# Value pages of a paged sample attention asked for by GpSimd's queue instead of SyncE's

## Chip, cores and metric

The kernel runs on one core of a Trainium2 chip. The metric is the device time of one execution in microseconds (us); the median of three runs of the kernel before is 1930.12 us (1930.09 to 1933.59). A core has TensorE (PE; its weight loads are listed as PEld), VectorE (DVE), ScalarE (ACT), GpSimd (POOL) and SyncE (SP), which here does nothing but ask for transfers and wait. The transfers run on 16 DMA engines.

## The reference, cut to what matters

One inference step of a small decoder: a gated short convolution layer, then a "forgetting attention" layer that reads shared keys and values, each followed by a gated embedding, and a last norm. There is a prompt of 1024 rows and a *sample* part: 8 sequences (batches) of 8 new rows each, which attend to 1024 cached rows apiece. The cached keys and values lie in a pool of pages of 128 rows; a page table names the eight pages of each batch. The change lies in the sample attention alone:

```python
k_past = cache_k[page_table].reshape(db, -1, N_HEADS, HEAD_DIM)      # 8 batches x 8 pages x 128 rows
v_past = cache_v[page_table].reshape(db, -1, N_HEADS, HEAD_DIM)
...
s_past = jnp.einsum('bqhd,bkhd->bhqk', q, k_past).astype(jnp.float32) * scale
s_past = s_past + cn_q + jnp.swapaxes(rest, 1, 2)[:, :, None, :]     # sums of log forget values
...                                                                  # s_new: against the 8 new rows, causal
p = jax.nn.softmax(jnp.concatenate([s_past, s_new], axis=-1), axis=-1)
o = jnp.einsum('bhqk,bkhd->bqhd', p[..., :P].astype(v_past.dtype), v_past)
o = o + jnp.einsum('bhqk,bkhd->bqhd', p[..., P:].astype(v_new.dtype), v_new)
```

All inputs and outputs are fp32. A page of keys, and one of values, is 128 rows x 1024 numbers: 512 KB.

## The kernel before, in words

Each engine has a program of its own, written out by hand; they are ordered by semaphores (`wait_ge`, `then_inc`). An instruction of an engine that waits holds up all behind it on that engine. The stages are: convolution layer, first embedding, keys and values, prompt attention (8 head pairs), **sample attention**, output projection, second embedding, norm. The sample attention goes from about 1449 to 1675 us of the profiled execution.

*Buffers of the sample attention.* `Kr` ("Kpages") holds eight key pages, `Vb` ("Vpages") eight value pages: one batch of each, and slot `pg` is used again for page `pg` of the next batch. `RB` holds the bias rows of two batches.

*TensorE, per batch b* (`sample_batch`, line 899): it turns key pages 3 to 7 with the identity (`k_turn`, line 808; the transposes are line 814), each in two halves, and between them forms the scores of finished pairs of pages (`s_scores`, line 833). `s_new` adds the scores against the new rows (lines 824 to 847). Then it turns pages 0 and 1 of batch b+1, turns the softmax weights of batch b (`s_p_turn`, lines 859 and 862), and multiplies them with the values (`s_values`, line 878: two halves of the heads, nine groups of four products each, the first eight groups over the value pages in their order, the ninth over the new rows). At its end it counts `s_pv`. Then come page 2 of batch b+1, the biases of batch b+1, and the transposes of the result (line 886).

*VectorE and ScalarE, per batch:* each copies one half of every turned key page out of PSUM (`keep_keys`: DVE line 1560, ACT line 1193). VectorE takes the maxima of the two halves of the heads (line 1578), with the copy of key page 0 of batch b+1 between the first and the second, and the copy of page 1 behind the second; ScalarE takes the exponentials (line 1207), one for each half. Then both copy the turned weights (lines 1591, 1216 and 1218), and VectorE scales the result (line 1599).

*SP, per batch* (`batch_pages`, line 431): first `value_pages(b)`, which loads the number of a page from the table into a register (`page`, line 292), waits once until the values of batch b-1 are done (`s_pv`, line 428), and asks for eight value pages (line 429). Behind it, for each of the eight key pages of batch b+1, it loads the page number, waits until TensorE has turned the page of batch b that lies in that slot (`s_kturn`), and asks (line 437). Then it asks for the bias rows of batch b+2 once the scores of batch b are done. After the seventh round it asks for the first two blocks of `w_out_b` (line 301), for the values of batch 7, and for the parked prompt output `Y` (line 451); once batch 7 is done it asks for `X` (line 456) and the remaining weights.

*The counters.* Those named in `LEAD` begin at the number written there, so that `START[name] + n` means "n more than at the start". `y_out` and `kv_out` say that the stores of the prompt attention have landed, whose SBUF the value pages take over.

*GpSimd* scales weights and softmax rows in the earlier stages, writes constants into `RB` before the sample attention (lines 561 to 565), and then has nothing to do until the last norm (line 569, from about 1800 us).

Of the kernel before, what the change touches and what calls it, by code (L numbers as in the profile page):

```python
# [27 lines left out]
SEQ, DB, DS = 1024, 8, 8  # L28
# [4 lines left out]
NPAIR = H // 2  # L33
PAGES, PAGE = 8, 128
# [50 lines left out]
START = {name: n for per in LEAD.values() for name, n in per.items()}  # L85


def f(x):

    return x.bitcast(F32)  # L90


def program(nc, a, o, d):

    es = ExitStack()
    with es:
        def sb(ctx, name, shape, dt=F32):
            return ctx.enter_context(nc.sbuf_tensor(name, shape, dt))

        def sem(name):  # L100
            return es.enter_context(nc.semaphore(name))
# [14 lines left out]
        pt = sb(es, "pt", [1, DB * PAGES], I32)  # L116
# [84 lines left out]
        Vb = sb(s2, "Vpages", [P, PAGES, D])  # L201
# [15 lines left out]
        def score_bank(qb):  # L217
# [2 lines left out]


        names = (
            "const_ready sp_step in_rows in_bf in_x0 in_x1 in_x2 w_in0 w_in1 w_gained w_hi w_split block_done act_evac dve_evac "
            "h_hi h_ready g_turned g_ready x_turned x_first x_act x_dve x_sum x_parked x_back y_back y_merged out_dma "
            "uc_turned uc_act uc_out f_raw f_abs f_ln f_lf f_turned f_nat f_aug f_augdma "
            "staged kv_turned kv_nat kv_out kq_hi kq_lo v_hi v_lo z_done "
# [7 lines left out]
        sems = {k: sem(k) for k in names}  # L234
# [19 lines left out]
        cv = a["cache_v"].rearrange("n s h d -> (n s) (h d)")  # L254
        cl = a["cache_logf"].rearrange("n s h -> (n s) h")
        last_page = a["cache_k"].shape[0] - 1
# [18 lines left out]
        def _(sp):  # L275
# [15 lines left out]
            def page(b, pg):  # L291
                v = sp.value_load(pt[0:1, bass.ds(PAGES * b + pg, 1)], min_val=0, max_val=last_page)  # L292
                return bass.ds(v * PAGE, PAGE)

            def load(n, par, src, proj=None, cols=P):

                sp.wait_ge(sems["w_split"], START["w_split"] + n - 1)
                sp.sem_inc(sems["sp_step"], 1)
                if proj is None:
                    for c in (0, 4):  # L300
                        sp.dma_start(raw[:, par, c:c + 4, 0:cols], src[:, c:c + 4, :]).then_inc(sems[f"w_in{par}"], 16)
                else:
                    sp.dma_start(raw[:, par, 0:KC, :], src).then_inc(sems[f"w_in{par}"], 16)
                    sp.dma_start(raw[:, par, KC:, :], proj).then_inc(sems[f"w_in{par}"], 16)
# [63 lines left out]
            def load_rest(b, par):  # L368
                for c in range(2):
                    sp.dma_start(f(RB[H * c:H * c + H, par, :]), d["rest"][bass.ds(H * b, H), c, :]).then_inc(sems[f"s_restin{par}"], 16)  # L370
# [49 lines left out]
            sp.wait_ge(sems["y_out"], START["y_out"] + 16 * NPAIR)  # L420
            sp.wait_ge(sems["kv_out"], START["kv_out"] + 64 * NPAIR)

            def value_pages(b):
                for pg in range(PAGES):
                    rows = page(b, pg)
                    if pg == 0:
                        sp.wait_ge(sems["s_pv"], START["s_pv"] + b)
                        sp.sem_inc(sems["sp_step"], 1)
                    sp.dma_start(Vb[:, pg, :], cv[rows, :]).then_inc(sems[f"v_in{pg}"], 16)

            def batch_pages(b, par, more_rest):
                value_pages(b)
                for pg in range(PAGES):
                    rows = page(b + 1, pg)
                    sp.wait_ge(sems["s_kturn"], 16 * b + 2 * pg + 2)
                    sp.sem_inc(sems["sp_step"], 1)
                    sp.dma_start(Kr[:, pg, :], ck[rows, :]).then_inc(sems[f"k_in{pg}"], 16)
                if more_rest:
                    sp.wait_ge(sems["s_all"], b + 1)
                    sp.sem_inc(sems["sp_step"], 1)  # L440
                    load_rest(b + 2, par)

            with sp.Fori(0, DB // 2 - 1) as i:
                for u in range(2):
                    batch_pages(2 * i + u, u, True)
            batch_pages(DB - 2, 0, False)
            for u in range(2):
                load(N_B2 + u, (N_B2 + u) % 2, w_out_b[:, :, P * u:P * u + P])
            value_pages(DB - 1)
            for k in range(KC):  # L450
                sp.dma_start(Y[:, k, 0:SEQ], d["y"][k]).then_inc(sems["y_back"], 16)

# [16 lines left out]
        def _(g):  # L469
# [23 lines left out]
            v = same[:, :].rearrange("p (b t) -> p b t", b=DB)  # L493
            g.affine_select(out=v, in_=v, compare_op=ALU.is_ge, fill=0.0, base=0,
                            pattern=[[-DS, DB], [0, DS]], channel_multiplier=1)
            v = maskQ[0:NS, :].rearrange("p (b t) -> p b t", b=DB)
# [65 lines left out]
            for b in range(2):  # L562
                g.memset(f(RB[64:P, b, :]), -1.0)
                g.drain()
                g.memset(f(RB[32:64, b, :]), -1.0)
                g.drain().then_inc(sems["s_ones"], 1)
            for k in range(KC):
                g.wait_ge(sems["n2_sq"], k + 1)
                g.tensor_scalar(X[:, k, :], X[:, k, :], GT[:, k, G_F:G_F + 1], 1.0, ALU.mult, ALU.mult).then_inc(sems["y_norm"], 1)
# [1107 lines left out]
```

## Time and profile before

| | |
|---|---|
| Median of three runs | 1930.12 us (1930.09 to 1933.59) |
| Profiled execution: time / span | 1929.29 us / 1927.5 us |
| Busy share of the span: PE, DVE, ACT, POOL | 90%, 46%, 37%, 14% |
| Mean granted TensorE clock | 0.952 |
| Key pages: transfers, each, median from request to landing | 64, 512 KB, 6.3 us |
| Value pages: the same | 64, 512 KB, 5.6 us |
| Sample attention, mean DMA rate from 1480.6 to 1645.9 us | 316 GB/s |

The median is taken over unprofiled runs, the span over one profiled execution, from its first to its last instruction; what lies around the span is 1929.29 - 1927.5 = 1.8 us. The busy share is an average over stages with different limits. In the granted clock 1.00 is 2.4 GHz and 0.50 is 1.2 GHz. In the lists, "Kpages<-in_cache_k" is a transfer or instruction that writes `Kpages` from `in_cache_k`; a letter L with a number is a line of the kernel; "SPq" is SP's sequencer; "<-" behind an idle time names what ended it.

### The profile page before, as it was taken

The page shows a single profiled execution, that of the slowest core. Times are in us where ns is not written, and L with a number is a line of the kernel's source. Part 1 is how long each engine was busy: PE and PEld are TensorE (multiplying, and loading weights), DVE is VectorE, ACT ScalarE, POOL GpSimd, SP SyncE. Part 2 cuts the span into 40 slices and gives each one's busy share as a digit, 9 for nine tenths or more (in the row PEclk, how much of TensorE's full clock was granted, in tenths as well). Part 3 has the DMA queues.
Part 4 walks back from the last instruction along what each step waited for, and adds up shares of the span by engine and source line. Part 5 has one row for each costly group of instructions (what it writes and reads, how often), then busy time and mean ns, then how long its engine had stood idle before and what let it go on. Part 6 is the DMA issues. An engine that isn't in the chain of part 4 may idle for free.

```text
span 1927.5 us, 32975 instructions
## 1 busy us (share of the span) xinstructions
PE 1737.7 (90%) x11725; PEld 1611.3 (84%) x11725; DVE 880.1 (46%) x1346; ACT 720.5 (37%) x1174; POOL 270.2 (14%) x234
## 2 busy tenths in 40 slices
PE   4799999999999948999999999999878788899997
PEld 2699999999989938988888888888755666799997
DVE  5722222224243374555655555555544444523443
ACT  3322222212043223555556565565632333402422
POOL 1311111110000021212222221222120000000110
PEclk8899999999999978999999999999969888899998
DMA  3011111111211023102111010211117888821102
GB/s 128 23 45 45 45 45 45 45 46 43 70 40 41 17 103 93 41 18 78 45 34 56 23 57 22 78 45 34 52 65 264 305 330 323 328 73 48 41 27 93
DMA packets 164071, 161.68 MB, mean 84 GB/s; under 512 B 18700, under 2 KB 140684, under 8 KB 163894
## 3 DMA queue, kind: packets, MB, share of 16 engines
q1 hardware_dynamic: 164022, 161.04, 25.2%
q8 instruction: 29, 0.48, 0.1%
q14 instruction: 20, 0.16, 0.0%
HBM read 137.21 MB, written 23.80 MB: 84 GB/s over the span
## 4 chain that ended last, share of the span: by engine, by line
PE 68%; DVE 9%; issue 6%; ACT 6%; DMA 3%; DVEq 3%; SPq 3%; ACTq 2%; POOL 0%; POOLq 0%
PE PS L585 14%; PE PS L587 14%; PE PS L586 14%; PE PS L708 4%; PE PS L710 4%; PE PS L709 4%; PE PS L767 3%; DMA Kpages<-in_cache_k 2%; PE PS L755 2%; DVE small L1433 2%; PE PS L878 2%; PE PS L738 2%; DVE pTl L1444 2%; SPq L292 1%; DVE Hlo L1285 1%
## 5 line engine op out<-in xcount | busy, mean ns | idle before, releaser
L585 PE MATMUL PS<-Hhi,w_hi 128*128 128x364 f32 (+1 forms) x1560 | 520.5, 334 | 55.5 <-DVE Hlo L1285 54.3
L587 PE MATMUL PS<-Hhi,w_lo 128*128 128x364 f32 (+1 forms) x1560 | 517.5, 332 | 0.0
L586 PE MATMUL PS<-Hlo,w_hi 128*128 128x364 f32 (+1 forms) x1560 | 517.4, 332 | 0.0
L585 PEld LDWEIGHTS PS<-Hhi,w_hi 128*128 128x128 f32 x1560 | 297.7, 191 | 62.8 <-issue 44.0
L587 PEld LDWEIGHTS PS<-Hhi,w_lo 128*128 128x128 f32 x1560 | 297.9, 191 | 0.0
L586 PEld LDWEIGHTS PS<-Hlo,w_hi 128*128 128x128 f32 x1560 | 297.9, 191 | 0.0
L708 PE MATMUL PS<-Hhi,w_hi 128*128 128x364 f32 (+1 forms) x768 | 274.5, 357 | 0.4 <-DVE w_lo L1256 0.4
L710 PE MATMUL PS<-Hhi,w_lo 128*128 128x364 f32 (+1 forms) x768 | 252.5, 329 | 0.0
L709 PE MATMUL PS<-Hlo,w_hi 128*128 128x364 f32 (+1 forms) x768 | 252.4, 329 | 0.0
L508 POOL TENSOR_TENSOR w_raw<-w_raw,GT 128x1024 f32<-128x1024 f32 x65 | 128.5, 1978 | 695.4 <-DMA w_raw<-in_w_kv 385.9
L961 ACT ACTIVATE w_hi<-w_raw 128x1024 fp32r<-128x1024 f32 (+1 forms) x97 | 105.8, 1091 | 295.6 <-PE PS L587 292.1
L1256 DVE TENSOR_TENSOR w_lo<-w_raw,w_hi 128x1024 fp32r<-128x1024 f32 (+1 forms) x97 | 126.0, 1299 | 141.1 <-ACT w_hi L961 137.6
L1444 DVE TENSOR_TENSOR pTl<-PS,pTh 128x512 fp32r<-128x512 f32 x192 | 103.5, 554 | 122.3 <-ACT pTh L1091 120.1
L1083 ACT ACTIVATE Pb<-PS,small 128x128 f32<-128x128 f32 (+7 forms) x128 | 94.8, 741 | 160.0 <-DVE small L1433 159.9
L708 PEld LDWEIGHTS PS<-Hhi,w_hi 128*128 128x128 f32 x768 | 147.2, 192 | 1.1 <-DVE w_lo L1256 0.6
L537 POOL TENSOR_SCALAR Pb<-Pb,small 128x128 f32<-128x128 f32 (+7 forms) x128 | 95.1, 747 | 377.2 <-DVE small L1438 377.2
L709 PEld LDWEIGHTS PS<-Hlo,w_hi 128*128 128x128 f32 x768 | 146.3, 190 | 0.0
L710 PEld LDWEIGHTS PS<-Hhi,w_lo 128*128 128x128 f32 x768 | 145.1, 189 | 0.0
L1091 ACT ACTIVATE pTh<-PS 128x512 fp32r<-128x512 f32 x192 | 89.8, 488 | 96.2 <-PE PS L755 92.9
L1433 DVE TENSOR_REDUCE small<-PS 128x1 f32<-128x128 f32 (+7 forms) x128 | 95.6, 748 | 36.6 <-PE PS L741 36.2
L814 PE MATMUL PS<-ident,Kpages 128*128 128x128 f32 x512 | 82.5, 313 | 29.0 <-DMA Kpages<-in_cache_k 25.9
L814 PEld LDWEIGHTS PS<-ident,Kpages 128*128 128x128 f32 x512 | 64.8, 159 | 49.4 <-issue 33.6
(221 smaller groups left out, 2236.7 us busy)
## 6 DMA issues: line engine op xcount, KB each, us to landing
Kpages<-in_cache_k SPq DMA_DIRECT2D x64, 512.0 KB, 6.3
Vpages<-in_cache_v SPq DMA_DIRECT2D x64, 512.0 KB, 5.6
w_raw<-in_w_in_a SPq DMA_DIRECT2D x64, 256.0 KB, 3.0
w_raw<-in_w_ple_gate SPq DMA_DIRECT2D x16, 512.0 KB, 3.7
w_raw<-in_w_kv SPq DMA_DIRECT2D x32, 256.0 KB, 3.1
w_raw<-in_w_in_b SPq DMA_DIRECT2D x32, 256.0 KB, 3.0
parked_x<-X SPq DMA_DIRECT2D x8, 544.0 KB, 5.2
X<-parked_x SPq DMA_DIRECT2D x8, 544.0 KB, 7.6
```

Source lines behind the costliest of these rows:

```text
L508: g.tensor_tensor(w, w, GT[:, :, r:r + 1].to_broadcast([P, KC, P]), ALU.mult).then_inc(sems["w_gained"], 1)
L585: mm(out, wh, hi[:, k, s:e], start=(k == 0), stop=False)
L586: mm(out, wh, lo[:, k, s:e], start=False, stop=False)
L587: last = mm(out, wl, hi[:, k, s:e], start=False, stop=(k == nk - 1))
L708: mm(out, wh, Hhi[:, k, s:e], start=(k == 0), stop=False)
L709: mm(out, wh, Hlo[:, k, s:e], start=False, stop=False)
L710: last = mm(out, wl, Hhi[:, k, s:e], start=False, stop=(k == KC - 1))
L814: last = tp(PS[:, c, (i % 4) * P:(i % 4 + 1) * P], Kr[:, pg, i * P:(i + 1) * P], ident[:, :])
L961: af(whi[:, par, 0:nk, :], raw[:, par, 0:nk, :], ACT.Copy).then_inc(sems["w_hi"], 1)
L1256: tt_(wlo[:, par, 0:nk, :], raw[:, par, 0:nk, :], f(whi[:, par, 0:nk, :]), ALU.subtract).then_inc(sems["w_split"], 1)
L1433: ve.reduce_max(small[:, qb:qb + 1], score_bank(qb)[:, 0:n], AXX, negate=True).then_inc(sems["rowmax"], 1)
L1444: tt_(pTl[:, kb % 2, q0 * P:512], PS[:, 5 + kb % 2, q0 * P:512], f(pTh[:, kb % 2, q0 * P:512]), ALU.subtract).then_inc(sems["p_lo"], 1)
```

## The change

The eight requests for the value pages of a batch leave SP's program and stand in a loop of GpSimd's, behind the constants and ahead of the final norm. The function is the same in both: page number from the table, one wait for the values of the batch before, a request per page, the same semaphores `v_in0` to `v_in7`. GpSimd's loop first waits for the page table and for the stores of the prompt attention, as SP does. SP keeps the key pages, the bias rows and all else, in the same order; where it asked for the values of batch 7, it now waits for the values of batch 6 before it asks for `Y`. `g_step` is a new counter, which nothing waits for.

```diff
-            def value_pages(b):
-                for pg in range(PAGES):
-                    rows = page(b, pg)
-                    if pg == 0:
-                        sp.wait_ge(sems["s_pv"], START["s_pv"] + b)
-                        sp.sem_inc(sems["sp_step"], 1)
-                    sp.dma_start(Vb[:, pg, :], cv[rows, :]).then_inc(sems[f"v_in{pg}"], 16)
-
             def batch_pages(b, par, more_rest):
-                value_pages(b)
                 for pg in range(PAGES):
                     rows = page(b + 1, pg)
                     sp.wait_ge(sems["s_kturn"], 16 * b + 2 * pg + 2)
...
             for u in range(2):
                 load(N_B2 + u, (N_B2 + u) % 2, w_out_b[:, :, P * u:P * u + P])
-            value_pages(DB - 1)
+            sp.wait_ge(sems["s_pv"], START["s_pv"] + DB - 1)
             for k in range(KC):
                 sp.dma_start(Y[:, k, 0:SEQ], d["y"][k]).then_inc(sems["y_back"], 16)
...
                 g.memset(f(RB[32:64, b, :]), -1.0)
                 g.drain().then_inc(sems["s_ones"], 1)
+
+            def value_pages(b):
+                for pg in range(PAGES):
+                    v = g.value_load(pt[0:1, bass.ds(PAGES * b + pg, 1)], min_val=0, max_val=last_page)
+                    if pg == 0:
+                        g.wait_ge(sems["s_pv"], START["s_pv"] + b)
+                        g.sem_inc(sems["g_step"], 1)
+                    g.dma_start(Vb[:, pg, :], cv[bass.ds(v * PAGE, PAGE), :]).then_inc(sems[f"v_in{pg}"], 16)
+
+            g.wait_ge(sems["s_table"], 16)
+            g.wait_ge(sems["y_out"], START["y_out"] + 16 * NPAIR)
+            g.wait_ge(sems["kv_out"], START["kv_out"] + 64 * NPAIR)
+            with g.Fori(0, DB) as b:
+                value_pages(b)
             for k in range(KC):
                 g.wait_ge(sems["n2_sq"], k + 1)
```

## Rows read from the trace of the kernel before

**Rows 1.** Issue list of the page: transfer, engine, count, size, median us to landing.
```profile
Kpages<-in_cache_k SPq DMA_DIRECT2D x64, 512.0 KB, 6.3
Vpages<-in_cache_v SPq DMA_DIRECT2D x64, 512.0 KB, 5.6
```
**Rows 2.** Chain of waits, sample stage: start us, us, what; value products of batches 0, 2, 6, 7.
```profile
1476.45 4.15 PE PS L878 x144
...
1532.38 4.14 PE PS L878 x144
...
1641.77 4.10 PE PS L878 x144
...
1666.14 4.74 PE PS L878 x144
```
**Rows 3.** Chain of waits through batch 3, from its first value request.
```profile
1536.86 0.35 SPq L429
...
1544.61 0.33 SPq L429
...
1545.94 6.27 DMA Kpages<-in_cache_k
...
1552.33 1.98 PE PS L814 x8
...
1554.42 0.69 DVE KT L1560
1555.12 1.13 DVEq L1579
...
1556.52 1.11 ACT Ps L1207
...
1558.09 1.11 PE PS L862 x8
...
1559.42 4.14 PE PS L878 x144
```
**Rows 4.** Waits, 1440 to 1680 us: who for whom, us in total, times, longest.
```profile
PE PS L814 <- DMA Kpages<-in_cache_k: 25.9, 7, 5.9
```
**Rows 5.** Timeline of PE, batch 3: start, us, what, [idle before <- what ended it].
```profile
1549.00 0.32 PE L847 MATMUL PS<-knT,qc 128*32 128x64 f32 x8
1552.33 3.96 PE L814 MATMUL PS<-ident,Kpages 128*128 128x128 f32 x16 [3.01 <-DMA Kpages<-in_cache_k]
```
**Rows 6.** Timeline of DVE in the same batch.
```profile
1549.59 1.21 DVE L1578 TENSOR_REDUCE small<-PS 128x1 f32<-128x1024 f32 x1
1550.88 0.16 DVE L1580 TENSOR_TENSOR small<-small 128x1 f32<-128x1 f32 x1
```
**Rows 7.** Instructions of the tile Vpages: ns min/median/max of a request; its landing in us.
```profile
L429 SPq DMA_DIRECT2D Vpages<-in_cache_v x64: 332/333/1566, 1452.5 to 1654.3; - x64
...
DMA to landing us min/median/max: 3.2/5.6/7.9
```
**Rows 8.** Groups of GpSimd's instructions: count, busy us, mean ns of one, idle before.
```profile
L515 POOL TENSOR_TENSOR scrZ<-X,scrC 128x1088 f32<-128x1088 f32 x8 | 20.4, 2545 | 101.5 <-DVEq L1281 73.6 <-DVE Hlo L1285 27.9
L563 POOL MEMSET RB<- 64x1088 f32 x2 | 2.0, 1004 | 0.3 <-issue 0.2
```
**Rows 9.** Stretches of batch 3: busy us of each engine, granted clock, DMA share, GB/s.
```profile
1538.00:1546.00 8.00, 8.00 (x83) 5.38 (x82) 3.53 (x7) 2.46 (x5) 0.00 (x0) 1.00 0.91 324
1549.30:1552.30 3.00, 0.01 (x3) 0.00 (x0) 1.58 (x3) 0.00 (x0) 0.00 (x0) 0.84 1.03 411
1552.30:1555.00 2.70, 2.67 (x12) 2.28 (x12) 0.58 (x1) 1.44 (x2) 0.00 (x0) 0.50 1.03 410
```
**Rows 10.** Timeline of PE in the last batch.
```profile
1662.04 3.68 PE L862 MATMUL PS<-ident,Ps 128*128 128x128 f32 x16 [3.33 <-ACTq L1208]
```
**Rows 11.** Timeline of SP behind batch 6: the reads of the parked output.
```profile
1654.63 4.12 SPq L451 DMA_DIRECT2D Y<-parked_y  x8
```

More of the change, by code:

```diff
@@ L222, in program @@
         names = (
-            "const_ready sp_step in_rows in_bf in_x0 in_x1 in_x2 w_in0 w_in1 w_gained w_hi w_split block_done act_evac dve_evac "
+            "const_ready sp_step g_step in_rows in_bf in_x0 in_x1 in_x2 w_in0 w_in1 w_gained w_hi w_split block_done act_evac dve_evac "
             "h_hi h_ready g_turned g_ready x_turned x_first x_act x_dve x_sum x_parked x_back y_back y_merged out_dma "
```

## The prediction, made before the changed kernel had run

> **What bounds the kernel now.** I read the issue list first, then the stretches, the chain of waits, and the timelines of the stage. The change touches the transfers of the sample attention's key and value pages, 512 KB each, all asked for by SP [rows 1]. Eight batches run one behind the other. I call the moment when a batch's last value product ends its *value end*: 1480.60 us for batch 0, 1645.87 for batch 6, 1670.88 for batch 7 [rows 2]. Six batches between the first two take (1645.87 - 1480.60) / 6 = 27.5 us each; the last takes 25.0.
>
> The chain inside one batch [rows 3] shows whose time this is. 0.3 us after a value end SP asks for eight value pages (first at 1536.86, eighth at 1544.61, so 1.11 us apart), and only then, at 1545.94, for the next batch's key page 0. That page lands after 6.27 us; TensorE turns it in 1.98 us, VectorE copies it (0.69), takes the second row maximum, which stands behind that copy in its program (1.13), ScalarE takes the exponentials (1.11), TensorE turns the weights (1.11) and forms the values (4.14). So 9.1 of 27.1 us are SP asking for pages that are needed 20 us later, ahead of a page that is needed at once. TensorE's wait for the key page is the stage's largest of its own: 25.9 us in seven batches, 0 to 6 [rows 4].
>
> **What the change takes away.** Keys and values get a queue each. Key slots 0 and 1 are free as soon as TensorE has turned their pages, which in program order is before the previous batch's values; SP then asks for their next pages some 10 us before that value end, not 9.5 us after it. Landing takes 6.3 us, so they lie in SBUF long before TensorE comes to them. The wait in this batch was 3.01 us [rows 5]. Without it: the last new-key score ends at 1549.3, the first row maximum and the minimum behind it at 1551.04 [rows 6], key page 0 has been turned meanwhile, and VectorE copies it from 1551.1 instead of 1554.42. All that follows moves by 3.3 us: the wait and 0.3. The batch then takes 27.1 - 3.3 = 23.8 us, bound by TensorE's own order and the softmax between VectorE and ScalarE. I count 25.9 us for the seven waits, the 0.3 once, 26.2 together, and don't rely on more.
>
> **What it adds: GpSimd asks.** Eight page numbers are loaded, and eight transfers asked for, by an engine that has nothing else to do in the stage (its last work before it is the memsets, its next the final norm). The sum needs s, the time from one of its requests to the next, and no row of before shows GpSimd asking for a transfer. On SP a page is 0.33 us of asking [rows 7] and so 0.78 of page number and registers. Lower bound: as on SP, s = 1.1. Upper bound: the slowest work that GpSimd does here, 2.55 us, in place of the 0.33: s = 3.3. GpSimd's shorter row, a memset that only writes 64x1088, takes 1.00 us [rows 8]; asking also reads no tile, so I take that one: s = 1.8.
>
> Values become late when 0.4 (wake and first load) + 7 s + landing exceeds the moment at which the eighth page is first read. That is after 28 of the 72 value products, 1.6 us into 4.14, with 2.5 us to go: 23.8 - 2.5 = 21.3 us after the previous value end. With a median landing of 5.6 us [rows 7] and s = 1.8 it lands at 18.6, hidden by 2.7 us. That cover is gone at s = 2.2; beyond it each batch costs 7 us per us of s.
>
> **What it adds: both streams at once.** With keys outstanding the 16 DMA engines ran full at 411 GB/s, while SP asked for values at 324 [rows 9]. A page is thus 0.524 MB / 411 = 1.28 us, and a batch (16 pages and 0.14 MB of bias rows) 8.53 / 411 = 20.7 us: it fits into 23.8 at 87%. Behind a value end, before the values are due, the engines must move eight value pages, six key pages and up to one and a half of the two behind them: 14 to 15.5 pages, 17.9 to 19.8 us, if both queues are served alike. Add 0.4 to the first request and 1.9 of bare latency (shortest landing 3.2 less 1.28): 20.2 to 22.1 us, against 21.3. So the last values are 0 to 0.8 us late. Batch 0 is alike: both streams start near 1452.5, and its value products would begin at 1476.45 - 4.1 = 1472.3.
>
> The Trainium skill ("DMA: Bandwidth & Descriptors", section "Issuing engines are not separate DMA queues") says that requests from several engines run on the same 16 DMA engines and that a second issuer saves only the issuing time, "usually small relative to the DMA itself". The first half agrees with the 411 GB/s; the second doesn't, since 9.1 us of asking stand in a chain of 27.1. By the rule the sum would be about nothing, 1930; by the rows it is 26 us.
>
> **The clock.** Behind a wait of about 3 us the granted clock falls to its lower level, 1.2 GHz (0.50 in the stretch in which TensorE turns the late page) [rows 9]. Without the wait TensorE has turned two key pages by 1551.4, and the first exponentials, 1.5 us long, end by 1552.6: gaps of some 1.2 us, for which I book no fall. The other bound is the last batch, which has no key wait but a gap of 3.33 us for ScalarE, and shows 3.68 us for sixteen turns and 4.74 for its values, against 2 x 1.11 and 4.14: 2.1 us dearer [rows 2, 10].
>
> **The last batch.** SP no longer asks for batch 7's values, so its eight reads of the parked attention output go out directly behind batch 6's value end, not 8.8 us later [rows 11]. Eight pages of each kind are 20.5 us, so the last value page lands by 22.8; it is read after about 20.3 + 1.8 = 22.1. I book nothing (bounds: loss 0.7, no gain, since the chain of that batch goes through the softmax).
>
> **Sum.** 26.2 less 4.2 (0.6 in each of seven batches for late values and an occasional slow clock) = 22.0. The profiled execution took 1929.29 us (span 1927.5 and 1.8 around it), so 1907.3; the median of the runs is 0.8 higher: 1908.
>
> **Rivals.** (a) *GpSimd asks slowly, and the wait moves from the keys to the values.* The place is the first value products. A batch is then 0.4 + 7 s + 5.6 + 2.5 = 8.5 + 7 s. Against 27.5 for batches 1 to 6, 25.0 for batch 7, and, with the first request at 1452.5 and a value end at 1480.6, 7 s - 20 for batch 0, the total is 56 s - 151: it turns into a loss at s = 2.7, and at the upper bound of 3.3 it costs 34 us: 1964. For it: no row shows the price, and GpSimd's rows reach 2.55. Against it: its writing row is 1.0. The Trainium skill ("SBUF — State Buffer", section "SBUF: two separate sides") gives a reason for a slow s: GpSimd writes the descriptors of its own transfers and is shut out while VectorE copies from SBUF to SBUF in its two-port mode. VectorE's copies in the stretch where values are asked for read PSUM (0.69 us each), so that wouldn't apply; no run here shows it yet.
>
> (b) *The transfers bind.* If the key queue is served first, the last value page lands after the whole batch: 0.4 + 20.7 + 1.9 = 23.0, value end 25.5. Six batches gain 2.0 each, batch 0 3.0, batch 7 loses 0.5: 14.5 gained, 1916. For it: 87% is close to full. Against it: six of the eight key pages can't be asked for before TensorE has turned their slots, which it does one by one over the 12.8 us up to the last score [rows 5].
>
> (c) *The clock falls anyway,* 2.1 us in seven batches: 26.2 - 14.7 = 11.5 gained, 1919. For it: the last batch. Against it: there TensorE has no key page to turn in the gap.
>
> (d) *Nothing measurable,* because s comes out near 2.7: about 1930.
>
> **How the numbers follow.** 0.2% (3.9 us) is what a measurement of this kernel can tell from no change. Forecast (1900 to 1914): 0.52; (b) 0.13; (c) 0.10; (a) 0.18; (d) 0.07. Faster 0.75, same 0.07, slower 0.18. The range runs from 1899, where no allowance is used and batch 7 gains too, to 1932, which takes in (b), (c) and (d) and leaves out (a).
>
> **What would show it.** The key-page wait of TensorE gone from the list of waits; value ends about 24 us apart; DMA near 350 GB/s over the stage; no value wait above 1 us; GpSimd's requests about 1.8 us apart. It is wrong if TensorE waits for value pages by more than 3 us a batch, or if the values' requests are more than 2.2 us apart.

## Result and profile after

The changed kernel takes 1943.15 us (median of 7 runs, 1937.49 to 1947.01), the kernel before 1930.12 (7 runs): ratio 1.0064, 95% interval 1.0048 to 1.0079. It is slower by 13 us in the medians; 22 us faster was forecast, and the range ended at 1932. The profiled execution took 1944.38 us, 15.1 more than that of before.

The sample attention gave the loss. The first fence is the chain of waits of the changed kernel (columns as in [rows 2, 3]): the last value page of a batch, from its request to its landing, then the rest of the value products (88 of their 144 instructions; L883 is line 878 of the kernel before), for batches 0, 1, 3, 6 and 7.

```profile
1461.93 17.56 DMA Vpages<-in_cache_v
1479.62 4.18 PE PS L883 x88
...
1493.32 15.92 DMA Vpages<-in_cache_v
1509.37 4.28 PE PS L883 x88
...
1551.52 15.69 DMA Vpages<-in_cache_v
1567.34 4.22 PE PS L883 x88
...
1639.64 13.79 DMA Vpages<-in_cache_v
1653.57 4.25 PE PS L883 x88
...
1667.30 14.96 DMA Vpages<-in_cache_v
1682.39 2.64 PE PS L883 x88
```

Where [rows 3] had SP's requests and a key page, the chain now has a value page that is 14 to 18 us under way. In batch 1 the last page lands 1509.24 - 1483.80 = 25.4 us behind the value end of batch 0; on the average of batches 1 to 7 it is 24.5 us. Value ends: 1483.80 us for batch 0 (before 1480.60, [rows 2]), 1657.82 for batch 6, 1685.03 for batch 7. Batches 1 to 6 take (1657.82 - 1483.80) / 6 = 29.0 us in place of 27.5, batch 7 27.2 in place of 25.0: 3.2 + 8.8 + 2.2 = 14.2 us of the 15.1. The waits of TensorE (answering to [rows 4]) say the same: no key page is left, value pages are. The second row is that of its weight loads, which run beside the products, so that the two don't add up.

```profile
PE PS L883 <- DMA Vpages<-in_cache_v: 26.7, 17, 3.0
...
PEld PS L883 <- DMA Vpages<-in_cache_v: 13.4, 9, 3.3
```

GpSimd's requests are not slow. Its timeline shows two in a row (0.53 us each), 1.24 us apart, and the tile's list a median landing of 10.5 us where [rows 7] had 5.6.

```profile
1542.78 0.53 POOL L565 DMA_DIRECT2D Vpages<-in_cache_v  x1 [19.11 <-PE PS L883]
1544.02 0.53 POOL L565 DMA_DIRECT2D Vpages<-in_cache_v  x1 [0.71 <-issue]
```
```profile
DMA to landing us min/median/max: 3.5/10.5/17.6
```

TensorE's timeline in batch 3 (answering to [rows 5]): the values begin at 1561.57, stop for pages 6 and 7 (1.52 and 2.30 us), and most of what is behind page 7 runs at the lower clock (0.50 from 1568.3 to 1571.3; 0.63 on the average of the last stretch in the fence after this one).

```profile
1561.57 1.52 PE L883 MATMUL PS<-Vpages,PsT 128*32 128x128 f32 x48
1564.62 0.42 PE L883 MATMUL PS<-Vpages,PsT 128*32 128x128 f32 x8 [1.52 <-DMA Vpages<-in_cache_v]
1567.34 0.43 PE L883 MATMUL PS<-Vpages,PsT 128*32 128x128 f32 x8 [2.30 <-DMA Vpages<-in_cache_v]
...
1567.77 3.34 PE L883 MATMUL PS<-Vpages,PsT 128*32 128x128 f32 x64
```

The stretches of that batch (columns as in [rows 9]; the batch before ends at 1542.04, the last value page lands at 1567.21), and then the two queues in three of these us: packets, MB, share of the 16 engines' time.

```profile
1542.30:1548.30 6.00, 6.00 (x60) 4.45 (x59) 2.90 (x7) 1.83 (x4) 2.59 (x5) 1.00 0.65 220
1548.30:1567.20 18.90, 12.88 (x170) 8.59 (x168) 8.61 (x18) 7.18 (x16) 1.63 (x4) 1.00 1.02 380
1567.20:1571.80 4.60, 4.46 (x91) 4.11 (x92) 0.22 (x1) 0.00 (x0) 0.00 (x0) 0.63 0.02 6
```
```profile
q0 software_dynamic: 178, 0.64, 52.6%
q1 hardware_dynamic: 167, 0.60, 49.6%
```

In these three us the two queues (q0 is GpSimd's, q1 SP's) get half of the engines each. Until the last value page has landed, 6.0 x 220 + 18.9 x 380 = 8.50 MB have moved: the batch's 16 pages and its bias rows, all of it. Then the engines stand still while TensorE forms the values (6 GB/s), since no slot is free to be filled. Before the change one queue moved the values first and the keys behind them, up to the end of the softmax (408 GB/s from 1555.0 to 1559.4 us, 87 in the 4.4 us of value products that follow).

### The profile page after: what moved, and what is told of

Read it like the earlier page. It is cut to its first block, busy times and chain, and to the rows that moved or that the text cites. A ratio compares the mean times of both kernels' runs of the same rounds, so it can differ in the third digit from the quotient of the medians.

```text
span 1942.8 us, 33041 instructions
## 1 busy us (share of the span) xinstructions
PE 1741.6 (90%) x11725; PEld 1610.0 (83%) x11725; DVE 879.4 (45%) x1346; ACT 721.7 (37%) x1174; POOL 304.7 (16%) x299
## 4 chain that ended last, share of the span: by engine, by line
PE 65%; DVE 9%; issue 7%; DMA 7%; ACT 5%; DVEq 2%; ACTq 2%; POOL 1%; POOLq 1%; SPq 0%
PE PS L590 14%; PE PS L592 14%; PE PS L591 14%; DMA Vpages<-in_cache_v 6%; PE PS L713 4%; PE PS L715 4%; PE PS L714 3%; PE PS L772 3%; PE PS L760 2%; DVE small L1438 2%; PE PS L883 2%; PE PS L743 2%; DVE pTl L1449 2%; DVE Hlo L1290 1%; PE PS L744 1%
## 5 line engine op out<-in xcount | busy, mean ns | idle before, releaser
L772 PE MATMUL PS<-pTh,VS 128*128 128x512 f32 x192 | 73.1, 381 | 35.2 <-DVE pTl L1449 34.8
L760 PE MATMUL PS<-ident,Pb 128*128 128x128 f32 x576 | 93.8, 283 | 6.7 <-POOL Pb L528 6.7
## 6 DMA issues: line engine op xcount, KB each, us to landing
Vpages<-in_cache_v POOLq DMA_DIRECT2D x64, 512.0 KB, 10.5
```

The lines of the kernel that those rows point to most:

```text
L760: last = tp(PS[:, 5 + kb % 2, qi * P:(qi + 1) * P], Pb[:, off:off + P], ident[:, :])
L772: last = mm(PS[:, 7, q0 * P:512], VS[:, kb, hh, :], x[:, kb % 2, q0 * P:512], start=(kb == 0 and x is pTh), stop=(kb == nkb - 1 and x is pTl))
```

## Experiments

**Theory A (order):** two queues share the engines alike, so values that are asked for last land with the last key page; a batch becomes the time of all its transfers plus the value products. **Theory B (queue):** GpSimd's queue is slow by itself. Each ratio is to the kernel before, measured beside it. A diff is against the changed kernel where nothing else is said, and "..." marks what is cut from it. The line numbers move with each kernel: L879, L888, L889 and L890 below are again the value products, L822 the transposes of key pages.

*Keys wait for the values.*

```diff
                     sp.wait_ge(sems["s_kturn"], 16 * b + 2 * pg + 2)
                     sp.sem_inc(sems["sp_step"], 1)
+                    if pg == 2:
+                        sp.wait_ge(sems["v_in7"], 16 * b + 16)
+                        sp.sem_inc(sems["sp_step"], 1)
```

> The changed kernel with one wait more: SP asks for key pages 2 to 7 of the next batch only when value page 7 of this batch has landed; key pages 0 and 1 are asked for as before. Theory A (order): the two queues share the 16 DMA engines half and half, so in the changed kernel the values land with the last key page, 24.5 us behind the value end before; alone on the engines they land by 8 x 1.28 + 3 = 13 us, the six key pages behind them by 13 + 8 + 3 = 24 us, when they begin to be needed. Batches of 24 us, TensorE's waits for values gone, 1908 us (1902 to 1914). Theory B (queue): GpSimd's queue itself delivers late, 10.5 us a page and 24 us for eight, whatever else runs; then the keys are asked for later and nothing is won: batches of 29 us or more, 1943 us or more.

Measured: 1928.72 us, ratio 0.9989 (0.9978 to 1.0): 14 us less than the change, but 21 more than the 1908. No value wait is left, but TensorE waits for keys again.

```profile
PE PS L822 <- DMA Kpages<-in_cache_k: 17.7, 16, 2.1
...
PEld PS L822 <- DMA Kpages<-in_cache_k: 8.5, 8, 2.1
```
```profile
1494.00:1496.00 2.00, 0.98 (x9) 0.74 (x8) 1.01 (x3) 1.52 (x5) 0.00 (x0) 1.00 0.80 307
1496.00:1498.00 2.00, 2.00 (x42) 1.76 (x45) 1.83 (x5) 1.81 (x4) 0.00 (x0) 1.00 0.04 14
1498.00:1500.00 2.00, 2.00 (x83) 2.00 (x78) 0.29 (x3) 0.00 (x0) 0.00 (x0) 1.00 0.57 145
```

The stretches show why: the last value page lands at 1497.65, and in the six us around it the engines lose 2 x (0.20 + 0.96 + 0.43) = 3.2 us, until the wait is over and SP's next requests bring data. The late keys run on into the next batch's values, whose last page lands 20 us behind the value end in this batch, not 13. Taking the competition away removes the value wait (A), but a wait between two queues costs a pause in the transfers; that part was not foreseen.

*SP alone, in another order* (against the kernel before).

```diff
             def batch_pages(b, par, more_rest):
-                value_pages(b)
                 for pg in range(PAGES):
+                    if pg == 2:
+                        value_pages(b)
                     rows = page(b + 1, pg)
```

> The kernel before, GpSimd asks for nothing: on SP alone, key pages 0 and 1 of the next batch are asked for ahead of this batch's values, pages 2 to 7 behind them. Theory A (order): one queue serves in its order, the late page 0 is gone and the values land by 12 us behind the value end; batches of 24 us, 1907 us (1902 to 1913), so the whole gain that the change was to bring lies in the order and none in a second queue. Theory B (queue): the values are not late either, since SP's queue delivers them, and it expects the same 1907. A third theory, that SP's time for asking (16 pages of 1.1 to 1.3 us, 19.8 us a batch) is what bounds the stage, expects no gain: 1930.

Measured: 1907.6 us, ratio 0.9874 (0.9857 to 0.989). The chain of waits has neither a transfer nor SP between two batches; value ends are 23.71 us apart.

```profile
1501.02 4.11 PE PS L879 x144
...
1524.73 4.11 PE PS L879 x144
...
1548.45 4.11 PE PS L879 x144
```
```profile
1505.13:1528.84 23.71, 21.38 (x317) 15.86 (x318) 11.74 (x25) 9.00 (x19) 0.00 (x0) 1.00 0.94 339
```

SP still spends 20 of these 23.7 us on its requests (the first at 1505.40, the last done at 1525.82), so they were never the bound; that they stood ahead of key page 0 was. This version beats both kernels, as does the one with all on GpSimd's queue below.

*The streams swapped* (GpSimd asks for keys, SP for values; against the kernel before).

```diff
             def batch_pages(b, par, more_rest):
                 value_pages(b)
-                for pg in range(PAGES):
-                    rows = page(b + 1, pg)
-                    sp.wait_ge(sems["s_kturn"], 16 * b + 2 * pg + 2)
-                    sp.sem_inc(sems["sp_step"], 1)
-                    sp.dma_start(Kr[:, pg, :], ck[rows, :]).then_inc(sems[f"k_in{pg}"], 16)
...
+            def key_pages(b):
+                for pg in range(PAGES):
+                    v = g.value_load(pt[0:1, bass.ds(PAGES * (b + 1) + pg, 1)], min_val=0, max_val=last_page)
+                    g.wait_ge(sems["s_kturn"], 16 * b + 2 * pg + 2)
+                    g.sem_inc(sems["g_step"], 1)
+                    g.dma_start(Kr[:, pg, :], ck[bass.ds(v * PAGE, PAGE), :]).then_inc(sems[f"kg_in{pg}"], 16)
...
+            with g.Fori(0, DB - 1) as b:
+                key_pages(b)
...
```

Here, and in the kernel with all on GpSimd's queue, TensorE's first two batches also stand outside its loop, so that batch 0's keys can keep a counter of their own.

> The two streams change queues: GpSimd asks for the key pages of batches 1 to 7, SP for the value pages. Theory A (order): which queue carries what doesn't matter, both are in flight at once and share the engines; the values still land last, some 24 us behind the value end: 1943 us (1936 to 1950). Theory B (queue): now the values come over the fast queue and land by 13 us, and the keys are the late ones; key pages 0 and 1 are asked for 10 us ahead, so batches of 24 to 26 us, 1906 to 1920 us.

Measured: 1926.64 us, ratio 0.9972 (0.9957 to 0.9986): outside both expectations. The values still land last, but sooner.

```profile
1509.82 2.64 PE PS L889 x88
...
1521.12 15.03 DMA Vpages<-in_cache_v
1536.30 2.64 PE PS L889 x88
```

In the batch shown, 1536.15 - 1512.46 = 23.7 us behind the value end; 23.4 on the average of batches 1 to 6, where the change has 24.5. In the first 9 us SP's values had 59.3% of the engines, GpSimd's values in the changed kernel 41.8%. And behind most of the landings TensorE kept its clock: 2.64 us in place of 4.2. In these six batches the sooner landings give 6.8 us and the clock 8.5. So the values still land last, as A says, but which queue carries what does matter, by 1943.15 - 1926.64 = 16.5 us, and A had expected no difference. Why SP's stream takes the larger share at first was not tested.

*Narrow keys.* This kernel leaves out three quarters of the key bytes of batches 1 to 7, and so of the function.

```diff
-                    sp.dma_start(Kr[:, pg, :], ck[rows, :]).then_inc(sems[f"k_in{pg}"], 16)
+                    sp.dma_start(Kr[:, pg, 0:D // 4], ck[rows, 0:D // 4]).then_inc(sems[f"k_in{pg}"], 16)
```

> The changed kernel, but the key pages of batches 1 to 7 bring only the first 256 of their 1024 columns (the others keep what batch 0 left), with every wait and every request as it was. Theory A (order): the keys take a quarter of the bytes, 1.05 MB beside 4.19; the values land by 3 + 5.2 / 0.41 = 16 us, before TensorE comes to them at 19.5; batches of 24 us, 1906 us (1902 to 1912). Theory B (queue): the values come at their own pace of 24 us for eight pages: 1940 us or more.

Measured: 1906.42 us, ratio 0.9867 (0.9851 to 0.9884), value ends again 23.71 us apart, and a median landing of a value page of 6.8 us where the change has 10.5:

```profile
1498.05 4.11 PE PS L883 x144
...
1521.75 4.11 PE PS L883 x144
```
```profile
DMA to landing us min/median/max: 3.5/6.8/15.0
```

With every wait and request unchanged, fewer key bytes make the values come in time. That is A; B is out.

*Two keys later.*

```diff
                     load_rest(b + 2, par)
+                    sp.wait_ge(sems["v_in7"], 16 * b + 16)
+                    sp.sem_inc(sems["sp_step"], 1)
```

> The changed kernel with one wait more: when SP has asked for a batch's bias rows, it waits until that batch's value page 7 has landed before it goes on to key pages 0 and 1 of the batch after next. In the changed kernel these two are asked for 15 us behind a value end and share the engines with the last value pages. Theory A (order): 14 pages in place of 16 lie ahead of the last value page, it lands 2.5 us sooner, 22 us behind the value end, and TensorE's wait is short enough to keep its clock: batches of 25 us in place of 29, 1912 us (1904 to 1922). Theory B (queue): GpSimd's queue delivers at its own pace, nothing changes: 1943 us.

Measured: 1937.76 us, ratio 1.0029 (1.0016 to 1.0042): a few us, not 30. The two keys didn't leave the competition, they changed ends: asked for just ahead of the value end, they move in its first us.

```profile
1512.60:1518.60 6.00, 6.00 (x58) 4.45 (x59) 3.13 (x7) 1.79 (x3) 2.35 (x5) 1.00 0.93 330
1518.60:1536.60 18.00, 13.13 (x172) 8.83 (x170) 8.61 (x18) 7.22 (x16) 1.88 (x4) 1.00 0.97 361
```

Until the landing at 1536.66 that is 6.0 x 330 + 18.0 x 361 = 8.48 MB, the whole batch once more. Which keys ride along makes little difference; B's 1943 is not met either.

*All on GpSimd's queue,* in the reordered kernel's order (`value_pages` and the rest of the loop as in the change and in the swapped kernel).

```diff
+            def key_pages(b):
+                for pg in range(PAGES):
+                    if pg == 2:
+                        value_pages(b)
...
-            with g.Fori(0, DB) as b:
-                value_pages(b)
+            with g.Fori(0, DB - 1) as b:
+                key_pages(b)
+            value_pages(DB - 1)
```

> Both streams on GpSimd's one queue, in the order of the reordered kernel (key pages 0 and 1 of the next batch, the values, key pages 2 to 7); SP asks for bias rows and all else; TensorE's first two batches stand outside its loop, so that batch 0's keys can keep a counter of their own. Theory A (order): one queue in the right order is enough, whichever engine holds it, 16 requests of 1.24 us fit into a batch: batches of 24 us, 1909 us (1903 to 1917). Theory B (queue): values over GpSimd's queue land late here too: 1930 us or more.

Measured: 1909.99 us, ratio 0.9893 (0.9876 to 0.9909):

```profile
1500.08 4.15 PE PS L890 x144
...
1523.87 4.21 PE PS L890 x144
```

GpSimd's queue carries both streams at 23.8 us a batch. One queue in the right order is enough, whichever engine holds it.

*The clock.* Three kernels fill TensorE's waits with products of zeros, and one repeats the change. The diff is that of the last of the three; the first had 24 narrower products ahead of each of pages 5, 6 and 7, the second 8 and 12 in place of 4 and 7.

```diff
+            g.memset(zero[:, :], 0.0)
...
+                        if s_ == 0 and pg in (6, 7):
+                            for _ in range((4, 7)[pg - 6]):
+                                mm(PS[:, 6, P:2 * P], zero[:, :], ones[:, :], start=False, stop=False)
                         if s_ == 0 and pg < PAGES:
                             pe.wait_ge(sems[f"v_in{pg}"], 16 * b + 16)
```

> The changed kernel, with 24 products of zeros (which change no number) in TensorE's program ahead of its waits for value pages 5, 6 and 7, some 1.4 us each, so that it works where it stood still. Theory A with the clock: value pages land as in the changed kernel, 24.5 us behind the value end, but the rest of the values (88 instructions) takes 2.6 us in place of 4.3, since the granted clock no longer falls to its lower level: 7 x 1.7 = 12 us less than the changed kernel, 1931 us (1925 to 1938). The rival, that the clock costs nothing because the transfers alone set the pace of the batch: 1943 us or more.

Measured: 1962.91 us, ratio 1.0173 (1.0156 to 1.0191). The 88 instructions took 2.4 to 2.5 us in most batches, but TensorE stopped within the batches for no cause that the profile names (its transposes of key pages 9.4 us in five such stops, against one of 2.5 in the changed kernel), and it reached the waits late. Why it stopped is open; this kernel decides nothing.

> The changed kernel with far fewer products of zeros (8 ahead of TensorE's wait for value page 6, 12 ahead of the one for page 7, 0.13 us each), since the 72 of the run before made TensorE stop for its own program elsewhere (gaps of 2.7 us put down to issue) and overshot the wait. Theory A with the clock: the last value page still lands 24.5 us behind a value end, and the 88 instructions behind it take 2.6 us in place of 4.3: 12 us less than the change as it is, 1931 us (1926 to 1937). The rival, that the clock costs nothing of its own: 1943 us.

Measured: 1944.86 us, ratio 1.0067 (1.005 to 1.0083). The clock held, but the zeros took 2.0 and 2.9 us, more than the waits:

```profile
1534.99 2.88 PE PS L882 x24
1537.87 2.54 PE PS L888 x88
```

> The changed kernel as it is, on the same chip as the run with the filled gaps. Every theory: 1943 us (1937 to 1947), values landing 24.5 us behind a value end, 88 instructions in some 4.3 us behind most of the landings.

Measured, on the chip of the kernel above and the one below: 1940.74 us, ratio 1.005 (1.0033 to 1.0067). In this execution the clock fell in four batches and held in four; the chain shows two of each:

```profile
1567.46 3.99 PE PS L883 x88
...
1596.29 4.06 PE PS L883 x88
...
1624.74 2.64 PE PS L883 x88
...
1651.21 2.64 PE PS L883 x88
```

> The changed kernel with 4 products of zeros ahead of TensorE's wait for value page 6 and 7 ahead of that for page 7. The run before showed 0.24 us for each of them where 0.13 was assumed, so its 20 took 4.9 us and were themselves the bound; these take 1.0 and 1.7 us, less than the waits that they stand in (1.0 to 1.5 and 2.0 to 2.5 us). Theory A with the clock: no batch falls to the lower clock, all show 2.6 us behind the last landing, batches of 27.2 us: 1931 us (1926 to 1936), steadier than the change as it is. The rival, that the clock costs nothing of its own: 1941 to 1943 us.

Measured: 1933.56 us, ratio 1.0018 (1.0009 to 1.0028). All batches show 2.6 us behind the landing, the last value pages of batches 1 to 5 land 24.4 to 25.2 us behind the value end as in the change (23.9 to 25.4), and the granted clock over the stage is 1.00, where the changed kernel has 0.93 (second row) and the kernel before 0.89 (third row):

```profile
1484.00:1658.00 174.00, 156.63 (x2132) 115.64 (x2130) 74.37 (x157) 57.97 (x120) 28.81 (x55) 1.00 0.85 317
...
1484.00:1658.00 174.00, 140.96 (x1899) 104.59 (x1898) 70.42 (x151) 54.06 (x114) 25.32 (x48) 0.93 0.80 294
...
1480.60:1645.90 165.30, 139.85 (x1897) 107.18 (x1898) 70.42 (x150) 53.38 (x114) 0.00 (x0) 0.89 0.85 316
```

The slow clock thus accounts for 7 to 10 us of the changed kernel (1940.74 and 1943.15 against 1933.56); with it gone, the change is still not faster than before. The clock alone can't be what separates the two kernels, since the one before, which is faster, has the lower clock in the stage.

## Why the prediction was wrong

- *What bounds before, and what the change takes away:* right. The key wait of [rows 4] is gone. In the reordered kernel, where nothing takes its place, a batch takes 23.71 us (23.8 worked out), and the kernel 1907.6 (1908 forecast, for another edit).
- *GpSimd asks:* right, if too dear. s is 1.24 us (1.1 to 3.3 allowed, 1.8 taken). Rival (a), which had all of the chance given to a slower kernel, put the new wait in the right place, but for a reason that didn't occur: it needed s above 2.7.
- *Both streams at once* is **the step that failed**. It let 14 to 15.5 pages go ahead of the last value page and had it land 20.2 to 22.1 us behind a value end, at most 0.8 us late; it landed after 24.5 on the average and 25.2 in batch 3, and the products waited 26.7 us for value pages in eight batches, more than the 3 us a batch that the prediction named as its sign of being wrong. Two parts of it failed. All 16 pages go ahead, as 8.50 MB show in the change and 8.48 with two keys moved: with equal shares, and the values asked for behind or beside the keys, the values end when everything ends. That makes 20.7 us at 411 GB/s in place of 17.9 to 19.8. And 411 GB/s were not held: in batch 3 the first 6 us moved 220 GB/s and the 18.9 behind them 380, which costs (411 - 220) x 6.0 / 411 + (411 - 380) x 18.9 / 411 = 4.2 us, where 2.3 were booked for the first request and the bare latency. Rival (b) had the right order of events (last value page at 23.0) but took the key queue as served first and still hoped for 1916.
- *The clock* was the second term mis-sized. Apart from 0.6 us a batch for late values and an occasional slow clock no fall was booked, on the ground that the key wait was gone; behind the value wait that came in its place it fell, and the 2.5 us behind the landing became 4.3 in most batches. 24.5 + 0.1 + 4.3 = 28.9 is the batch of 29.0.
- *The last batch:* 2.2 us lost (0 to 0.7 allowed), by the same late landing, at 24.4 us; there the clock held (2.64 us).
- *The page's rule.* The Trainium skill ("DMA: Bandwidth & Descriptors", section "Issuing engines are not separate DMA queues"), by which a second issuer saves only the time of asking, was set aside because SP's asking stood in the chain. It was right as far as it goes: SP's asking takes as long in the reordered kernel, which has the whole gain. By it the sum was about nothing, 1930; that the second queue would cost 13 us, it doesn't say. The Trainium skill's section "Queues, rings and completion order", on the same page, says that each DMA engine takes turns between the queues that have work; the trace agrees, 52.6% to 49.6%. The forecast used equal shares, but didn't follow them to the last value page.

## What to carry to other kernels

A second queue added no transfer rate here (414 GB/s with both queues full, 411 with one); it gave up the order. Where two streams together need most of a stage (here 20.7 of 23.7 us), keep them in one queue in the order in which they are needed, and move the one late request ahead of the bulk. When a wait goes, work out the landing of the *last* page of the other stream with all transfers of the batch ahead of it, and count the buffer's dead time: a slot that is freed only at the batch's end makes transfer and use add up.

## What was not expected of the hardware

- A request for 512 KB costs GpSimd 0.53 us, and with its page number 1.24 us; on SP it is 0.33 and 1.11.
- A TensorE wait of 2 to 3 us doesn't always cost the clock: in the repeated change it fell behind waits of 1.90, 2.02, 2.23 and 2.54 us for value page 7 and held behind 2.29 and 2.57. Since each fall costs 1.3 to 2.3 us, this may be why the changed kernel's runs spread over 9.5 us. The mean granted clock of the runs goes with it (0.959 in the fastest, 0.953 in the slowest), but it was not tested by itself.
- An fp32 product of 128x128 by 128x128 is listed as two instructions and took 0.24 us, where a transpose of that shape is one instruction of 0.13.
